# Two transformer blocks on one core: twenty expert places, small products dealt out between large ones, two weight chunks together at branch norms, and a memory norm in later groups

## The reference, cut to what matters

```python
# first block, layer i = 0, 1
u = rms_norm(h, mix_pre_g[i])
y = dilated_attention(u) if i == 0 else differential_attention(u)   # mixers "A" and "B"
h = h + rms_norm(y, mix_post_g[i])
u = rms_norm(h, mem_pre_g[i])
k, v = split(rms_norm(mem, mem_kv_g[i]) @ x_wkv[i])                 # 256 memory rows
h = h + rms_norm(softmax(heads(u @ x_wq[i]) @ k.T) @ v @ x_wo[i], mem_post_g[i])
u = rms_norm(h, ffn_pre_g[i])
g, up = split(u @ w_gate_up[i])                                     # 2 x 2816 columns
h = h + rms_norm((silu(g) * up) @ w_down[i], ffn_post_g[i])

# second block, layer l = 0, 1
dq, dk, dv, dz, db, da, sq, sk, sv, iq, ik, iw = split(h @ w_in[l])
dq, dk, dv = split(silu(causal_conv4(concat(dq, dk, dv))))          # 4 heads of 128
o_dn = gated_delta_rule(l2norm(dq), l2norm(dk), dv, gates(db, da))  # norm, times silu(dz)
score = sum_h(relu(rope(iq_h) @ rope(ik).T / 8) * iw_h)             # 8 heads of 64
keep = top_k(causal(score), 64)                                     # 64 keys for a query
o_sa = softmax(rope(sq) @ rope(sk).T / 8, only where keep) @ sv     # 8 heads of 64
h = layer_norm(alpha * h + concat(o_dn, o_sa) @ w_out[l])
e1, e2, gate = router(h)                                            # 2 of 32 experts a token
ffn = sum over both: gate * ((silu(h @ w1[e]) * (h @ w3[e])) @ w2[e])
h = layer_norm(alpha * h + ffn)
```

## Time and profile before

| | us |
|---|---|
| median of 3 runs | 2313.65 (2312.2 to 2320.56) |
| profiled execution | 2318.01 |
| its span, first to last instruction | 2316.0 |
| PE busy | 2088.0 (90%), 14359 instructions |
| DVE, ACT, POOL busy | 936.2, 741.7, 697.7 |
| DMA | 404.59 MB, mean 175 GB/s |

### The profile page before, as it was taken

The page is one execution under the profiler, slowest core; times in us unless marked ns, Lnnn a source line. Parts: engine busy times, 40 slices in busy tenths (PEclk is TensorE's granted clock), DMA queues, the critical chain, the costliest instruction groups (busy, mean ns, idle before and its releaser), DMA issues.

```text
span 2316.0 us, 36763 instructions
## 1 busy us (share of the span) xinstructions
PE 2088.0 (90%) x14359; PEld 1653.1 (71%) x14359; DVE 936.2 (40%) x1872; ACT 741.7 (32%) x1184; POOL 697.7 (30%) x558
## 2 busy tenths in 40 slices
PE   6999999999999999999999985769999999869866
PEld 5889989989899899977687752324777687734423
DVE  4652346525535266156452431111385442512212
ACT  5555443445535433323122121212222221112211
POOL 5566737856766388400020000000000020000000
PEclk9999999999999999999988997979999898989978
DMA  6335335543353355534100479994522002596794
GB/s 215 110 110 164 128 118 191 170 141 128 128 163 129 110 182 179 167 112 146 56 18 1 182 284 421 389 420 161 181 85 98 37 1 110 210 379 276 299 420 167
DMA packets 196124, 404.59 MB, mean 175 GB/s; under 512 B 18499, under 2 KB 143830, under 8 KB 171270
## 3 DMA queue, kind: packets, MB, share of 16 engines
q1 hardware_dynamic: 192230, 388.85, 45.7%
q0 software_dynamic: 3744, 13.63, 1.6%
HBM read 399.18 MB, written 3.28 MB: 174 GB/s over the span
## 4 chain that ended last, share of the span: by engine, by line
PE 50%; DMA 9%; DVE 3%; ACT 1%; issue 1%; ACTq 1%; DVEq 1%; SPq 0%
PE ps L1291 9%; PE ps L1616 8%; DMA weight_ring<-in_w 5%; DMA acts<-in_w 4%; PE ps L982 3%; PE ps L983 3%; PE ps L984 3%; PE ps L1527 3%; PE ps L1638 2%; PE ps L1040 2%; PE ps L1382 1%; PE ps L1381 1%; PE ps L1467 1%; PE ps L1474 1%; PE ps L1646 1%
## 5 line engine op out<-in xcount | busy, mean ns | idle before, releaser
L2104 POOL TENSOR_TENSOR weight_ring<-weight_ring 128x512 fp32r<-128x512 f32 (+1 forms) x466 | 629.3, 1384 | 331.9 <-ACT weight_ring L1712 312.5
L982 PE MATMUL ps<-weight_ring 128*128 128x256 f32 x1824 | 533.6, 293 | 27.0 <-DVE acts L2183 17.6
L984 PE MATMUL ps<-weight_ring 128*128 128x256 f32 x1568 | 442.6, 282 | 0.0
L983 PE MATMUL ps<-acts,weight_ring 128*128 128x256 f32 x1472 | 418.8, 284 | 0.0
L982 PEld LDWEIGHTS ps<-weight_ring 128*128 128x128 f32 x1824 | 348.4, 191 | 41.9 <-issue 40.2
L984 PEld LDWEIGHTS ps<-weight_ring 128*128 128x128 f32 x1568 | 301.8, 192 | 0.0
L983 PEld LDWEIGHTS ps<-acts,weight_ring 128*128 128x128 f32 x1472 | 282.3, 192 | 2.2 <-issue 1.7
L1616 PE MATMUL ps<-weight_ring,x_g 128*32 128x512 f32 x1056 | 188.5, 654 | 89.7 <-DMA acts<-in_w 53.2
L1712 ACT ACTIVATE weight_ring<-weight_ring 128x2048 fp32r<-128x2048 f32 x128 | 239.1, 1883 | 91.3 <-PE ps L984 81.4
L1291 PE MATMUL ps<-acts,weight_ring 128*128 128x272 f32 x896 | 218.8, 405 | 7.8 <-ACTq L1962 5.0
L2126 POOL CAST row_of<-slot_token 128x1 uint32 (+1 forms) x26 | 5.0, 191 | 690.2 <-PE ps L1594 448.0
(11 more groups left out here) (455 smaller groups left out, 3692.2 us busy)
## 6 DMA issues: line engine op xcount, KB each, us to landing
weight_ring<-in_w SPq DMA_DIRECT2D x132, 1024.0 KB, 19.8
weight_ring<-in_w_gate_up SPq DMA_DIRECT2D x44, 1024.0 KB, 5.1
acts<-in_w SPq DMA_DIRECT2D x40, 1024.0 KB, 25.4
weight_ring<-in_w_in SPq DMA_DIRECT2D x16, 2048.0 KB, 9.0
h_area<-in_w SPq DMA_DIRECT2D x20, 1024.0 KB, 28.0
weight_ring<-in_x_wkv SPq DMA_DIRECT2D x16, 1024.0 KB, 5.3
weight_ring<-in_w_down SPq DMA_DIRECT2D x16, 1024.0 KB, 4.9
weight_ring<-in_a_w_in SPq DMA_DIRECT2D x12, 1024.0 KB, 7.2
```

The source lines that it names most:

```text
L982: nc.tensor.matmul(o, wh, xh, start=start, stop=False)
L983: nc.tensor.matmul(o, wh, xr, start=False, stop=False)
L984: return nc.tensor.matmul(o, wr, xh, start=False, stop=stop)
L2104: nc.gpsimd.tensor_tensor(r12(w), w, r12(high[:, n % HIGH, part]).bitcast(F32), ALU.subtract).then_inc(rest_ready, 1)
```

## The change

- **Experts.** 20 places in place of 18. The two new ones (`last_pair`) lie where the second table, the narrow weights and the router's weights were. Small constants that the experts need move to the first table (897 to 1030 columns), and the second table is loaded anew for layer 1, behind that layer's narrow weights; PE and DVE wait for it there. Loads 18 and 19 wait only for the ranks' tile "rk".
- **Memory.** In mixer A the transposes go to group 1, the sum to group 2, ACT's copies and squares with them, the multiplication on DVE to the end of group 3.
- **Branch norms.** `project_together` computes two chunks pair by pair of u tiles: g 0 with u 0 in both layers, qk 0 with qk 4 in mixer B. There the norm of the first group stands behind both.
- **Second block.** New orders: iq 0, ik, then iq 1 to 3, with the narrow products in three pieces and the rotations between; index products in sixes with a "c" tile behind each six; sq and sk's first projections ahead of and between the l2 sums; the scores of groups 0 and 1 each between pieces of the preparation of the last 16 tokens; in score groups 6 and 7 the four heads' products one after another and then their masks, and in the values likewise.

The diff, cut to its core:

```diff
-TABLES = dict(ident=128, rot1=128, rot2=128, invf=1, maskA=512)
+TABLES = dict(ident=128, rot1=128, rot2=128, invf=1, maskA=512, iota=32, group=32, edges=9, count=MAX_STEPS, slot_of=4, token=3)
...
-        XS = 18
+        XS = 20
...
-        tab2 = sb("tables2", [P, W2], stack=second)
-        small_w = sb("small_w", [P, KT, 144], stack=second)
-        router_w = sb("router_w", [P, KT, 36], stack=second)
+        lent = ExitStack()
+        tab2 = sb("tables2", [P, W2], stack=lent)
+        small_w = sb("small_w", [P, KT, 144], stack=lent)
+        router_w = sb("router_w", [P, KT, 36], stack=lent)
+        lent.close()
+        last_pair = sb("last_pair", [P, 4096], stack=second)
...
+            if expert_slot(g, m) >= 18:
+                at = (expert_slot(g, m) - 18) * XW
+                return last_pair[:, at:at + n * XW]
...
-                order = [("qk", 0, 0), ("norm",), ("qk", 0, 1), ("qk", 4, 0), ("memT",), ("qk", 4, 1), ("mem",), ("v", 0, 0), ("rot", 0), ("rtok",),
+                order = [("qk", 0, 0), ("norm",), ("qk", 0, 1), ("qk", 4, 0), ("qk", 4, 1), ("v", 0, 0), ("rot", 0), ("rtok",),
                          ("v", 0, 1), ("rot", 4)]
...
-                    order += [S[0], S[1], q0, q1, T[0], T[1], S[2], S[3], k0, V[0], V[1], *rot_q, k1, T[2], T[3], v0, V[2], V[3], *rot_k, v1]
+                    order += [S[0], S[1], q0, q1, *({1: [("memT",)], 2: [("mem",)]}.get(g, [])), T[0], T[1], S[2], S[3], k0, V[0], V[1], *rot_q, k1, T[2], T[3], v0, V[2], V[3], *rot_k, v1]
...
-                    if g == 2:
+                    if g == 3:
...
-        INDEX, ROT = [("iq", 4), ("ik", 1)], [("sq", 4), ("sk", 4)]
+        INDEX = [("iq", 0), ("ik", 0), ("iq", 1), ("iq", 2), ("iq", 3)]
+        ROT = [(nm, i) for nm in ("sq", "sk") for i in range(4)]
+        IX = [(n, h) for n in range(3) for h in range(SH)]
...
+        def rot_order():
+
+            order = rot_tiles(ROT)
+            sums = [("l2", None, i, None) for i in range(8)]
+            return order[:5] + sums[:4] + order[5:7] + sums[4:] + order[7:]
...
+                            elif g == 1 and m == 6:
+                                b, u = tiles[("rk", l)]
+                                sp.wait_ge(full[b], u)
...
-                        b, u = tiles[("rt", 0)]
-                        sp.wait_ge(full[b], u)
                         narrow_weights(1)
+                        sp.dma_start(tab2[:, :], A["tables2"]).then_inc(const2_in[1], 16)
...
+            def project_together(keys, src):
+
+                w = [split_weights(*key) for key in keys]
+                banks = [begin(*key) for key in keys]
+                for q in range(KT // 2):
+                    for key, (wh, wr), b in zip(keys, w, banks):
+                        for nt in range(2):
+                            for k in (2 * q, 2 * q + 1):
+                                if nt == 0:
+                                    rest_of(key, k)
+                                at = k * 256 + nt * P
+                                last = split_products(ps[:, b, nt * S1:(nt + 1) * S1], (wh[:, at:at + P], wr[:, at:at + P]), src(k),
+                                                      start=(k == 0 and nt == 0), stop=(k == KT - 1 and nt == 1))
+                        if q == KT // 2 - 1:
+                            last.then_inc(full[b], 1)
...
+                    if what == "qk" and kind == "B" and at[0] in (0, 4):
+                        if at == [0, 0]:
+                            project_together([("qk", l, 0), ("qk", l, 4)], src)
...
-                    project(("g", l, c), src)
-                    project(("u", l, c), src)
+                    if c == 0:
+                        project_together([("g", l, 0), ("u", l, 0)], src)
+                    else:
+                        project(("g", l, c), src)
+                        project(("u", l, c), src)
...
-                pe.wait_ge(rot_done, 13 * l + 5)
-                for n, (t0, L, W) in enumerate(QUERY):
-                    for h in range(SH):
-                        p0 = HD * (h % 2)
-                        b = begin("ix", l, n, h)
-                        nc.tensor.matmul(ps[0:L, b, 0:W], iq[p0:p0 + HD, h // 2, t0:t0 + L], ik[p0:p0 + HD, 0, 0:W],
-                                         start=True, stop=True).then_inc(full[b], 1)
-                for nm, at in PROJ:
+                pe.wait_ge(const2_in[l], 16 if l else 16 * 10)
+
+                for m, (n, h) in enumerate(IX):
+                    t0, L, W = QUERY[n]
+                    if n == 0 and h % 2 == 0:
+                        pe.wait_ge(rot_done, 13 * l + 2 + h // 2)
+                    p0 = HD * (h % 2)
+                    b = begin("ix", l, n, h)
+                    nc.tensor.matmul(ps[0:L, b, 0:W], iq[p0:p0 + HD, h // 2, t0:t0 + L], ik[p0:p0 + HD, 0, 0:W],
+                                     start=True, stop=True).then_inc(full[b], 1)
+                    if m % 6 == 5:
+                        project2(("c", l, m // 6), weights("dq", l), m // 6 * P, 512)
+                for nm, at in PROJ[1:]:
                     s = weights(nm, l)
                     for i in range(4):
                         project2(("c", l, at + i), s, i * P, 512)
 
-                for i in range(8):
...
-                    for j in range(H):
-                        p0 = HD * odd
-                        o = ps[0:L, b, j * W:j * W + W] if n < 2 else ps[32 * j:32 * j + 32, b, 0:W]
-                        nc.tensor.matmul(o, qs[p0:p0 + HD, c0 + j, t0:t0 + L], ks[p0:p0 + HD, c0 + j, 0:W], start=True, stop=False)
-                        last = nc.tensor.matmul(o, ident[0:L, 0:L], score[0:L, n, 0:W], start=False, stop=True)
+                    p0 = HD * odd
+                    o = [ps[0:L, b, j * W:j * W + W] if n < 2 else ps[32 * j:32 * j + 32, b, 0:W] for j in range(H)]
+                    for some in ([[j] for j in range(H)] if n < 2 else [range(H)]):
+                        for j in some:
+                            nc.tensor.matmul(o[j], qs[p0:p0 + HD, c0 + j, t0:t0 + L], ks[p0:p0 + HD, c0 + j, 0:W], start=True, stop=False)
+                        for j in some:
+                            last = nc.tensor.matmul(o[j], ident[0:L, 0:L], score[0:L, n, 0:W], start=False, stop=True)
...
+                prepare(0, PREP)
+                prepare(1, PREP)
+                pe.wait_ge(rot_done, 13 * l + 13)
+                pe.wait_ge(mask_ready, l + 1)
+                pe.wait_ge(vs_ready, 3 * l + 3)
+                scores_of(0)
+                prepare(2, PREP[:2])
+                scores_of(1)
+                prepare(2, PREP[2:])
+                side_work("prep2")
```

More of the change, by code:

```diff
@@ L563, in mixer_scalar_order @@
                 order += [S[0], S[1], before, q]
+                if kind == "A" and g < 3:
+                    order += [("memT",)] if g == 1 else [("mem",)]
                 if kind == "A":
@@ L739, in rot_tiles @@
         def rot_tiles(which):
[L741 removed]
+            names = list(which)
             base = 0 if which is INDEX else 5
```

194 lines of the change are left out of this document (100 added, 94 removed).

## The result

| | before | changed |
|---|---|---|
| median of 4 runs, us | 2313.81 (2312.2 to 2320.56) | 2223.52 (2216.83 to 2226.11) |
| profiled execution, us | 2318.01 | 2216.83 |
| span, us | 2316.0 | 2215.0 |
| PE busy, us | 2088.0 | 2023.3 |
| mean granted clock | 0.936 | 0.955 |

The changed kernel is faster: ratio 0.9598, 95% interval 0.9573 to 0.9623, or 90 us by the medians.

The account below looks back on a forecast made before the run. TensorE (PE) bounds the kernel, through idle, half clock and waits for expert weights. Terms −5.0−19.7−37.8−21.8 = −84.3 us take the profiled 2318.0 to 2233.7, or 2229 from the median; range 2207 to 2268.

Parts of the forecast that it names:

- Memory: Mixer A, memory norm moved to later groups: −5.0 us in sum, bounds −9 and +1.
- The work comes back in groups that have no hole: Mixer A: moved memory work costs transposes +1.9, sum +3.6, ACT's work between probabilities of groups 1 and 2 +2.0 and +1.0.
- Two chunks at the norms: Branch norms, two chunks together: −7.2 at g0 and u0 in each layer, −5.3 in mixer B, sum −19.7 us.
- half is idle and half the clock: Products of g0 and u0: of the 7.2 us gained, half was idle and half the clock, 3.4 us lost.
- −0.9 index products (3.4 us of them slow, not all bound by PE): Second block's front: index products take 9.77 us and gain 0.9 a layer; the idle ahead of them gains 1.7.
- The narrow products: Second block's front: small products dealt out between projections avoid a half-clock projection behind them, −1.6 us a layer.
- l2 sums and rotations: Second block: sq and sk's first projections beside ACT's squares, 12.7 us against 20.9, −8.2 a layer; −4.8 if the clock falls.
- Heads: Second block, scores 6 and 7: four heads overlap in column strips, factor 3.7, −2.8 and −5.4 us a layer.
- The rival's mechanism: Experts: second pass waits for gathered rows, so places give nothing, +21.8 us, 2251; chance 0.24 together with the half-clock rival.
- Half clock did not follow everywhere: Rival: half clock follows small products wherever they go, 2251 us; chance 0.24 together with the rival on experts.
- The slower one: Rival: full clock stays away behind dealt-out scores until head scores 7, 60 us take 120 a layer, 2349; chance 0.04.
- the four for "wrong": Over 5 us idle before first memory product; PE waiting for GpSimd's remainder; half clock over 20 us; DMA wait before step 1.

Follow-up runs that it names:

- Experiment 10: Changed kernel plus products of no use in PE's two idles of mixer A (seven before the first scores, nine before the first memory product): 2216.55 us, ratio 0.9583.
- experiment 4: Changed kernel with the branch norms' two chunks one after the other and three products of no use ahead of each later pair of u tiles: 2235.3 us, ratio 0.9661.
- experiment 6: Changed kernel with the 24 index products in one block again and all convolution tiles behind them: 2231.4 us, ratio 0.9635.
- Experiment 5: Changed kernel with the 32 narrow products in one piece again, behind iq 0 and ik: 2224.2 us, ratio 0.9605.
- experiment 7: Changed kernel with the eight l2 sums ahead of sq and sk again: 2238.5 us, ratio 0.9659.
- experiment 8: Changed kernel with scores and values of groups 6 and 7 head by head again: 2249.3 us, ratio 0.9721.
- experiment 9: Changed kernel with scores 0 and 1 together again ahead of the preparation of the last tokens: 2222.6 us, ratio 0.9601.
- experiment 1: Changed kernel with 18 places for expert loads in place of 20: 2248.1 us, ratio 0.9716.
- experiments 2 (the first): Changed kernel with the memory's transposes, sum and norm back where they were; first of its two runs: 2228.3 us, ratio 0.9634.
- experiments 3: Changed kernel with each branch norm's two chunks computed one after the other again, at all three places: 2236.0 us, ratio 0.966.

## Why the prediction was right, step by step

**Right in sum, with errors that cancelled.** By places the profiles show −2.6 + 20.1 + 64.6 + 23.0 − 4.1 = 101 us, where the forecast had 5.0 + 19.7 + 37.8 + 21.8 = 84.3. About 11 of the 17 between them are the two profiles' distance from their medians. By the medians 90.3 us were gained, 6.0 more than forecast: the heads, the index products and the experts gave more, the memory, the narrow products and the l2 sums less, and the sum is better than its terms.

- **Memory: −5.0 forecast, +2 to +2.6 measured, outside its bound of +1 (by the start of the first gate's products).** The step that failed is "The work comes back in groups that have no hole" with its +2.0 and +1.0. The head did lose 11.1 (13.0 forecast), group 2 grew by 4.7 (4.6 forecast), group 3 shrank by 3.5 as said, and the first memory product waited 5.09 in place of 1.98, the 3.0 as said. But group 1 grew by 8.5 and not by 3.9: the rotations' chain on DVE ends 4.02 us after PE's last product, and behind that idle the half-clock stretch of 6.8 us, which had stood in the head, fell on products bound by PE. In group 1 PE was idle for 3.1 us, and 6.5 us at half clock cost another 3.2. Experiment 10 shows that idle filled and the group 2.2 us shorter.
- **Two chunks at the norms: −19.7 forecast, −20.1 measured,** each place within 0.2. Wrong was "half is idle and half the clock": experiment 4 gave 1.7 us of clock. GpSimd's lead sufficed: PE waits for it behind none of the three places. What the sum left out is a loss of 3.3 us behind mixer B's place (last point).
- **Front of the second block: the step "−0.9 index products (3.4 us of them slow, not all bound by PE)" was mis-sized.** With the idle ahead of them they gave 6.0 us a layer (2.16 + 9.77 less 5.9; experiment 6 has 11.8 again), where 1.7 and 0.9 were forecast. The trace of before had it: 9.77 us for 24 products that need 5.9, in a block where PE looked 100% busy. I took the extra for clock, and it was mostly the wait for banks: the last ten products, at clock 1.00, took 5.71 us, and six of the kind that eight of them are take 1.56 now.
- **The narrow products: −1.6 forecast; not shown.** Experiment 5 moved nothing that could be measured, and the slow projection came back in 12 of the 22 layers with the new order. That it is gone from both layers here is part of the profile's luck.
- **l2 sums and rotations: −8.2 forecast, −6.9 measured** (experiment 7).
- **Heads: −2.8 and −5.4 forecast; experiment 8 measures 25.8 in both layers, 12.9 each.** The factor 3.7 for strips, taken from the experts, held at 3.6. Scores 6 and 7 gave 3.3 and 6.2, a little more than forecast. Left out of the sum were the values (L1457, before L1411), the term that the forecast put at nothing by not naming it: in layer 0 24 records went from 2.3 to 0.7 us and again 24 from 3.2 to 1.0, 3.8 together.
- **Scores 0 and 1 dealt out: 0 forecast, nothing measurable** (experiment 9).
- **Experts: −21.8 forecast, −23.0 in the profiles and 24.6 by experiment 1.** The first late load was waited for 7.48 us, forecast 7.5. The rival's mechanism, rows gathered too late, came with 1.8 us.
- **The rivals.** Half clock did not follow everywhere: with 0.936 and 0.955 as means it went from some 300 us to 200 in the profiles. The slower one did not come: the clock was full again when the X products had begun, 6.8 and 20.5 us long at half.
- **Signs.** Those for "right" came: first mixer scores at 44.87, g 0 and u 0 in 11.40 with no idle inside, clock 1.00 behind "sm" (in this profile), scores 6 and 7 at 1.26 and 1.25, 7.48 at the first late load. But three of the four for "wrong" came too, each by a little: 5.09 us ahead of the first memory product, 20.5 us in a row at half clock about layer 1's preparation, and 1.8 us of waiting for gathered rows. The sum was right all the same, so these signs were set too near to what was forecast.
- **The range.** "Half of what the better bounds add" to the forecast is 12.4 us and gives 2217; the 2207 on record is nearly all of it. The measured 2223.5 lies inside either way.
- **Between the norms** the changed kernel lost 3.3 us from mixer B's first scores to the second gate: 0.8 in the first group and 2.4 to 2.5 behind the fourth group's scores, which lie 163.5 us ahead of that gate in place of 161.0. It is no single case. Of the ten profiles with two chunks together, seven have the longer stretch (experiment 7's has 9 us more on top, by the instruction of the last section) and three, of experiments 2 (the first), 6 and 10, have 161.0 or 161.1, as have all four with chunks apart. In the long ones the half clock lies elsewhere (607.7 and twice near 640, 3.4 us each, in place of 6.8 in a row), and PE waits 2.33 us in place of 0.7 to 0.9 for DVE at 644.9 (L2220). So in most runs the pairs' 20.1 us are 17 by the second gate. Why the clock falls elsewhere with the chunks together is open.

## What to carry to other kernels

Ask of a block in which PE looks busy how long the same products take where nothing limits them: 24 index products at 9.8 us against 5.9 hid an error of 3.4 us a layer here, and large independent products laid between small ones took it all. Fill a wait with useful products of another chunk rather than with filler: keeping the clock up was worth 1.7 us where useful work was worth 5.7. And products that use 32 columns each want their four column strips in turn, scores and values alike; that gave 26 us (experiment 8) for a change of the order of two loops.

## What the runs showed of the hardware

**A vector instruction can be kept waiting through a whole run of GpSimd.** The scaling of probabilities on DVE has these durations in the kernel of experiment 10 (ns, least, median, most; 64 instructions):

```profile
L2325 DVE TENSOR_SCALAR probs<-probs,small x64: 340/354/8553, 48.3 to 742.9; 128x256 f32<-128x256 f32 x64
```

and so it looks in its timelines of DVE, PE and GpSimd:

```profile
240.84 8.82 DVE L2325 TENSOR_SCALAR probs<-probs,small 128x256 f32<-128x256 f32 x2
...
249.71 1.11 PE L1122 MATMUL ps<-tables,probs 128*128 128x128 f32 x4 [6.58 <-DVE probs L2325]
...
231.85 17.39 POOL L2166 TENSOR_TENSOR weight_ring<-weight_ring 128x512 fp32r<-128x512 f32 x14
```

The first of the two scalings (240.84 to 249.39) began while one of GpSimd's 14 products (17.39 / 14 = 1.24 us each) ran, and ended only when the whole run had (231.85 + 17.39 = 249.24); PE waited 6.58 us. The same, 8.55 us, stands in the profile of experiment 7 at 716.3; none of the twelve other profiles has a scaling over 1.53 us. In all fourteen, 433 scalings began while a GpSimd product ran: 406 ended 0.15 to 0.29 us after that product, 25 after the next one, and these two after the whole run. Both of the two began 0.23 us into a product; dozens of others began 0.21 to 0.26 us into one and waited only for it, so what sets them apart is open. That this is what makes some runs of one kernel 10 us longer is likely from these two, and not tested. The Trainium skill (SBUF — State Buffer, section SBUF: two separate sides) says that GpSimd and certain kinds of DVE instruction share a pair of ports, and that whichever starts first holds it for the whole instruction while the other is blocked. The 406 scalings agree with that. The two long ones were blocked for more than one instruction: six more of GpSimd's, which stood behind the running one, went ahead.

**The slow clock comes behind PE's idles** (0.82 over g 0 and u 0 with four idles of 1.0 to 1.7 us, 1.00 with them filled, experiments 3 and 4), **and also behind busy stretches of small products** (5.04 us in place of 3.83 behind 4.6 us of narrow products with no idle, experiment 5), and not every time: the same order had it in one layer and not in the other (experiment 5). A single profile's slow stretch is no evidence for an order.
